# Two attentions of an eight-layer forward pass: order of scores, projections and last down products

## What is computed

```python
# differential attention: 8 heads, two score maps each, head width 64, value width 128
s = einsum(q, k) * scale + bias            # blocks of 128 queries; mask by chunks of 64
p = softmax(s)
o = (p[0] - lam * p[1]) @ v
o = rmsnorm(o, sub_g) * (1 - lambda_init)
y = o @ w_out
# stick-breaking attention: 16 heads of 64; keys and values from a norm of their own
z = q @ k.T / 8                            # strictly causal
log1m = where(mask, -softplus(z), 0)
a = exp(log_sigmoid(z) + sum of log1m to the right)
y = (a @ v) @ w_o
```

## Time and profile before

| | us |
|---|---|
| median of 3 runs | 1122.97 (1122.48 to 1123.53) |
| the profiled execution | 1124.0 |
| its span, first to last instruction | 1122.1 |
| TensorE busy in it | 1086.4 (97%) |
| VectorE busy | 757.3 (67%) |
| ScalarE busy | 633.9 (56%) |
| POOL busy | 127.8 (11%) |
| mean granted clock of TensorE | 0.991 |

### The profile page before, as it was taken

How to read it: one execution, slowest core, us unless ns; L and a number is a source line. 1 busy time by engine, 2 the same in 40 slices (tenths; PEclk the granted TensorE clock), 3 DMA queues, 4 the chain that set the end, 5 groups by cost and what they waited for, 6 DMA issues and landing times.

```text
span 1122.1 us, 15867 instructions
## 1 busy us (share of the span) xinstructions
PE 1086.4 (97%) x6474; PEld 949.8 (85%) x6474; DVE 757.3 (67%) x883; ACT 633.9 (56%) x848; POOL 127.8 (11%) x131
## 2 busy tenths in 40 slices
PE   9999999999999989999997999999999998999997
PEld 8979888887899788888876888888899878888886
DVE  6877876767776668766767765656675546755554
ACT  7656755656555656665565343435568765443532
POOL 0001332120021164312200000000000000000000
PEclk9999999999999989999999999999999999999999
DMA  9836676553544455555542556464363333655551
GB/s 345 307 123 238 221 253 216 168 183 138 192 152 146 150 207 174 204 185 187 192 146 76 207 192 220 160 216 169 132 225 126 104 113 145 213 183 197 178 187 38
DMA packets 31143, 202.23 MB, mean 180 GB/s; under 512 B 3640, under 2 KB 3808, under 8 KB 8544
## 3 DMA queue, kind: packets, MB, share of 16 engines
q1 hardware_dynamic: 28032, 189.16, 48.0%
q0 software_dynamic: 3040, 12.07, 3.2%
HBM read 200.15 MB, written 2.63 MB: 181 GB/s over the span
## 4 chain that ended last, share of the span: by engine, by line
PE 78%; DVE 11%; ACT 4%; issue 3%; POOL 2%; DMA 1%; SPq 0%; DVEq 0%; ACTq 0%; POOLq 0%
PE wk L621 20%; PE wk L623 10%; PE acc L595 8%; PE acc L597 8%; PE acc L596 8%; PE wk L644 4%; DVE w_lo L296 4%; PE wk L595 3%; PE wk L597 3%; PE wk L596 3%; ACT w_hi L287 2%; PE wk L653 1%; DVE x L1469 1%; DVE region L1663 1%; PE acc L779 1%
## 5 line engine op out<-in xcount | busy, mean ns | idle before, releaser
L296 DVE TENSOR_TENSOR w_lo<-raw,w_hi 128x2048 fp32r<-128x2048 f32 x168 | 384.3, 2292 | 74.6 <-ACT w_hi L287 68.6
L621 PE MATMUL wk<-a_hl,w_hi 128*128 128x512 f32 x1024 | 365.2, 400 | 3.7 <-DVE region L1771 1.9
L287 ACT ACTIVATE w_hi<-raw 128x2048 fp32r<-128x2048 f32 x173 | 329.5, 1907 | 13.2 <-DMA raw<-ws 12.5
L623 PE MATMUL wk<-a_hl,w_lo 128*128 128x256 f32 x1024 | 288.0, 281 | 0.0
L621 PEld LDWEIGHTS wk<-a_hl,w_hi 128*128 128x128 f32 x1024 | 193.1, 189 | 52.5 <-DVE region L1653 3.2
L623 PEld LDWEIGHTS wk<-a_hl,w_lo 128*128 128x128 f32 x1024 | 194.1, 190 | 1.5
L595 PE MATMUL acc<-w_hi,b_hl 128*128 128x512 f32 x432 | 169.4, 392 | 1.3 <-DVE w_lo L296 1.3
L596 PE MATMUL acc<-w_lo,b_hl 128*128 128x512 f32 x432 | 168.5, 390 | 0.0
L597 PE MATMUL acc<-w_hi,b_hl 128*128 128x512 f32 x432 | 168.4, 390 | 0.0
L1363 ACT ACTIVATE region<-wk 128x512 f32<-128x512 f32 x30 | 17.9, 596 | 159.8 <-PE wk L623 156.5
L595 PEld LDWEIGHTS acc<-w_hi,b_hl 128*128 128x128 f32 x432 | 81.1, 188 | 19.6 <-DVE w_lo L296 2.1
(11 more groups left out here) (258 smaller groups left out, 1653.7 us busy)
## 6 DMA issues: line engine op xcount, KB each, us to landing
raw<-ws SPq DMA_DIRECT2D x173, 1024.0 KB, 4.9
gain<-gains POOLq DMA_DIRECT2D x13, 512.0 KB, 4.8
raw<-ws SPq DMA_DIRECT2D x8, 256.0 KB, 6.2
region<-rows SPq DMA_DIRECT2D x1, 1664.0 KB, 9.7
lines_dram<-line_dram POOLq DMA_DIRECT2D x1, 1536.0 KB, 8.7
bias<-gains POOLq DMA_DIRECT2D x3, 512.0 KB, 6.9
region<-xT SPq DMA_DIRECT2D x4, 256.0 KB, 5.0
x<-x_rows SPq DMA_DIRECT2D x1, 1024.0 KB, 7.2
```

What stands on the lines that cost most here:

```text
L287: act.activation(w_hi[:, u % HIGH, :], raw[:, u % RAW, :], ACT.Copy).then_inc(hi_ready, 1)
L296: dve.tensor_tensor(w_lo[:, u % LOW, :], raw[:, u % RAW, :], w_hi[:, u % HIGH, :].bitcast(F32), ALU.subtract).then_inc(lo_ready, 1)
L621: pe.matmul(banks[:, m, :], wh[:, k, c], a_hl[:, k, :, :].rearrange("p e t -> p (e t)"), start=k == 0, stop=False, skip_group_check=True)
L623: mm = pe.matmul(banks[:, m, T:2 * T], wl[:, k, c], a_hi[:, k, :], start=False, stop=k == DT - 1, skip_group_check=True)
```

## The change

- **Scores inside the value projections.** In both attentions the scores stand in the middle of a value unit and no longer behind it; units are cut with `feat_part` and `token_part`. Differential attention's first round has an order of its own (`diff_first`): scores(0) ahead of the low products of v, scores(1) in the middle of the next query unit. VectorE's and ScalarE's lists are rewritten to it.
- **Queries of four heads first.** Stick-breaking attention takes its units in the order q0, q1, k0, v0, k1, v1, q2, k2, v2, q3, k3, v3 (`STICK_UNITS`), and its junction prepares the keys' input later.
- **Last four downs by token halves.** `down_tokens` does one half of the tokens of a down unit; half 0 of all four comes before half 1 of the last three. The low part of the last unit of each attention goes to spare memory (`SPARE`). `by_threes` now holds for these junctions too, so half 0 is turned ahead of the last half unit, and the low split of the next sublayer's first unit moves from ahead of the junction into it.
- **Mean squares without divisions.** With den the sum of exponentials, the old steps computed (ss / den / den / 128 + eps) ^ -0.5 / den on POOL in five instructions. The new ones compute (ss / 128 + eps den^2) ^ -0.5, two on VectorE and the power on POOL.

The diff, cut to its core:

```diff
+STICK_UNITS = (("q", 0), ("q", 1), ("k", 0), ("v", 0), ("k", 1), ("v", 1), ("q", 2), ("k", 2), ("v", 2), ("q", 3),
+               ("k", 3), ("v", 3))
+STICK_MID = {3: 0, 4: 1, 5: 2, 6: 3, 8: 4, 9: 5}
+STICK_END = {10: 6, 11: 7}
...
+        SPARE = {U_DIFF + 15: o_lo_t[:, :, :].rearrange("p k t -> p (k t)"),
+                 U_STICK + 15: b_hl[:, 0:DT // 2, :, :].rearrange("p k e t -> p (k e t)")}
+        def low_of(u):
+            return SPARE[u] if u in SPARE else w_lo[:, u % LOW, :]
...
+            if u == U_STICK + 15:
+                dve.wait_ge(unit_done, U_STICK + 12)
+            elif u >= LOW and u not in SPARE:
...
-            return n not in (J_DIFF, J_POOL, J_STICK)
+            return n != J_POOL
...
-                pool.wait_ge(o_squared, 4 * (j + 1))
-                over = rden[:, :, :].rearrange("p e (n m) -> p e n m", m=2)[:, :, :, 0]
-                four = lambda t: t[:, c].rearrange("p (e n) -> p e n", e=2)
-                pool.tensor_tensor(four(o_ms), four(o_ss), over, ALU.mult).then_inc(o_mean, 1)
-                pool.wait_ge(o_mean, 4 * j + 1)
-                pool.tensor_tensor(four(o_ms), four(o_ms), over, ALU.mult).then_inc(o_mean, 1)
-                pool.wait_ge(o_mean, 4 * j + 2)
-                pool.tensor_scalar(o_ms[:, c], o_ms[:, c], 1.0 / P, EPS, ALU.mult, ALU.add).then_inc(o_mean, 1)
-                pool.wait_ge(o_mean, 4 * j + 3)
-                pool.tensor_tensor(o_rs[:, c], o_ms[:, c], minus_half[:, :], ALU.pow).then_inc(o_mean, 1)
-                pool.wait_ge(o_mean, 4 * j + 4)
-                pool.tensor_tensor(four(o_rs), four(o_rs), over, ALU.mult).then_inc(o_rms, 1)
+                pool.wait_ge(o_mean, 2 * j + 2)
+                pool.tensor_tensor(o_rs[:, c], o_ms[:, c], minus_half[:, :], ALU.pow).then_inc(o_rms, 1)
...
+            def down_tokens(n, u, h, pair, res, first=False):
+                last = u == LAST[n]
+                if h == 0:
+                    pe.wait_ge(lo_ready, u + 1)
+                for f in range(2):
+                    for kk in range(2):
+                        mm = down_half(u, h, kk, f, *pair, res, first and kk == 0, last and kk == 1)
+                    if last:
+                        mm.then_inc(unit_done if h and f else res_done, 1)
+                if h and not last:
+                    mm.then_inc(unit_done, 1)
...
+            def diff_first(base):
+                half_pair(base, wk[:, 0:2, :], J_FFN0, 0)
+                half_pair(base + 1, wk[:, 2:4, :], J_FFN0, 0)
+                turn_half(J_FFN0, 1)
+                half_token(base + 2, acc[:, 3, :], J_FFN0, 0, a_hi, a_lo)
+                half_pair(base, wk[:, 0:2, :], J_FFN0, 1)
+                low_pair(base, wk[:, 0:2, :])
+                half_pair(base + 1, wk[:, 2:4, :], J_FFN0, 1)
+                low_pair(base + 1, wk[:, 2:4, :])
+                half_token(base + 2, acc[:, 3, :], J_FFN0, 1, a_hi, a_lo)
+                pe.wait_ge(dq_ready, 1)
+                pe.wait_ge(dk_ready, 1)
+                diff_scores(0)
+                low_token(base + 2, acc[:, 3, :], a_hi)
+                feat_part(base + 3, 0, range(0, 4))
+                pe.wait_ge(dv_ready, 2)
+                diff_scores(1)
+                feat_part(base + 3, 0, range(4, DT))
+            diff_first(U_DIFF)
             for j in range(1, 4):
-                projections(U_DIFF, j, 0, dreleased)
-                outputs_pair(j - 1)
-                projections(U_DIFF, j, 1, dreleased)
+                u = U_DIFF + 3 * j
+                if j > 1:
+                    pe.wait_ge(dq_ready, j)
+                    feat_part(u, 0, range(DT))
+                pe.wait_ge(dk_ready, j)
+                if j > 1:
+                    outputs_pair(j - 1)
+                    feat_part(u + 1, 1, range(DT))
+                else:
+                    diff_turn(0)
+                    feat_part(u + 1, 1, range(0, 4))
+                    diff_av(0)
+                    diff_turn(1)
+                    feat_part(u + 1, 1, range(4, 6))
+                    diff_av(1)
+                    feat_part(u + 1, 1, range(6, DT))
+                pe.wait_ge(dv_ready, 2 * j)
+                token_part(u + 2, 2, 0, range(0, 4), a_hi, a_lo)
                 diff_back(j - 1)
-                projections(U_DIFF, j, 2, dreleased)
-                scores_pair(j)
-            pe.wait_ge(dv_ready, 8)
-            unit_down(U_DIFF + 12, *b_pair(0), True, res=wk)
+                token_part(u + 2, 2, 0, range(4, DT), a_hi, a_lo)
+                pe.wait_ge(dq_ready, j + 1)
+                pe.wait_ge(dk_ready, j + 1)
+                diff_scores(2 * j)
+                diff_scores(2 * j + 1)
+                token_part(u + 2, 2, 1, range(DT), a_hi, a_lo)
+            u = U_DIFF + 12
+            down_tokens(J_DIFF, u, 0, b_pair(0), wk, True)
+            down_tokens(J_DIFF, u + 1, 0, b_pair(1), wk)
             outputs_pair(3)
-            unit_down(U_DIFF + 13, *b_pair(1), False, res=wk)
+            down_tokens(J_DIFF, u + 2, 0, b_pair(2), wk)
             diff_back(3)
-            last_downs(J_DIFF, U_DIFF + 14, (b_pair(2), b_pair(3)), (None, (o_lo, 8)), res=wk)
+            down_tokens(J_DIFF, u, 1, b_pair(0), wk, True)
+            pe.wait_ge(o_lo, 8)
+            down_tokens(J_DIFF, u + 3, 0, b_pair(3), wk)
+            down_tokens(J_DIFF, u + 1, 1, b_pair(1), wk)
+            down_tokens(J_DIFF, u + 2, 1, b_pair(2), wk)
+            turn_half(J_DIFF, 0)
+            down_tokens(J_DIFF, u + 3, 1, b_pair(3), wk)
...
+            def stick_first(base):
+                q0, q1, k0 = wk[:, 0:2, :], wk[:, 2:4, :], acc[:, 2:4, :]
+                half_pair(base, q0, J_MLP0, 0)
+                turn_half_kv(0)
+                half_pair(base + 1, q1, J_MLP0, 0)
+                pe.wait_ge(blo_ready, 2)
+                turn_half(J_MLP0, 1)
+                half_pair(base + 2, k0, J_MLP0, 0, b_hl, True)
+                half_pair(base, q0, J_MLP0, 1)
+                turn_half_kv(1)
+                low_pair(base, q0)
+                half_pair(base + 1, q1, J_MLP0, 1)
+                low_pair(base + 1, q1)
+                half_pair(base + 2, k0, J_MLP0, 1, b_hl, True)
+                low_pair(base + 2, k0, b_hi)
...
+            for c in range(3, 12):
+                if c == 3:
+                    pe.wait_ge(sq_ready, 2)
+                stick_unit(c, 0)
+                if c in STICK_MID:
+                    stick_there(STICK_MID[c])
+                    stick_step(STICK_MID[c])
+                stick_unit(c, 1)
+                if c in STICK_END:
+                    stick_there(STICK_END[c])
+                    stick_step(STICK_END[c])...
+                if n == J_MLP0:
+                    split_hi(act, last + 3)
                 if by_threes(n):
                     input_hi(0)
                 result_squares(1)
                 if not by_threes(n):
                     input_hi(0)
+                x_squares(1)
                 if n == J_MLP0:
                     kv_hi(0)
-                x_squares(1)
-                if n == J_FFN1:
+                    input_hi(1)
...
-            for j in range(4):
+            low_copy(U_DIFF, wk[:, 0:2, :], diff_low[:, 0, :, :], d_low)
+            low_copy(U_DIFF + 1, wk[:, 2:4, :], diff_low[:, 1, :, :], d_low)
+            split_hi(act, U_DIFF + 3)
+            diff_exp(0)
+            split_hi(act, U_DIFF + 4)
+            token_copy(U_DIFF + 2, 0, 3, av, ACT.Copy, dv_ready, src=acc)
+            diff_exp(1)
+            split_hi(act, U_DIFF + 5)
+            for j in range(1, 4):
...
-                token_copy(u + 2, j, 2 if j else 3, av, ACT.Copy, dv_ready, src=wk if j else acc)
-                split_hi(act, u + 2 + CUT)
+                diff_o_hi(j - 1)
                 diff_exp(2 * j)
                 diff_exp(2 * j + 1)
+                token_copy(u + 2, j, 2, av, ACT.Copy, dv_ready)
+                split_hi(act, u + 2 + CUT)
...
-                if n == J_MLP0:
-                    kv_lo(0)
                 if not by_threes(n):
                     input_lo(0)
                 next_input(1)
                 if n == J_MLP0:
+                    kv_lo(0)
+                input_lo(1)
+                if n == J_MLP0:
                     kv_input(1)
-                input_lo(1)
...
+                dve.scalar_tensor_tensor(out=four(o_rs), in0=under, scalar=EPS, in1=under, op0=ALU.mult, op1=ALU.mult)                   .then_inc(o_mean, 1)
...
+                dve.scalar_tensor_tensor(out=four(o_ms), in0=four(o_ss), scalar=1.0 / P, in1=four(o_rs), op0=ALU.mult,
+                                         op1=ALU.add).then_inc(o_mean, 1)
...
-            for j in range(4):
+            feat_sum(wk[:, 0:2, :], diff_low[:, 0, :, :], d_low, 1, qT[:, 0:2, :], dq_ready)
+            split_lo(dve, U_DIFF + 3)
+            feat_sum(wk[:, 2:4, :], diff_low[:, 1, :, :], d_low, 2, kT[:, 0:2, :], dk_ready)
+            diff_bias(0)
+            split_lo(dve, U_DIFF + 4)
```

(19 more changed lines are left out.)

## The result

| | before | after |
|---|---|---|
| median of the runs, us | 1123.25 (1122.48 to 1124.06, 4 runs) | 1134.76 (1133.18 to 1136.95, 4 runs) |
| ratio, 95% interval | | 1.0105 (1.009 to 1.012) |
| profiled execution, us | 1124.0 | 1136.95 |
| its span | 1122.1 | 1135.1 |
| mean granted clock | 0.991 | 0.986 |

The change makes the kernel 11.5 us slower. Forecast was 6.2 slower with 1133 as upper end: the sign was right, the time 5.6 us too low and outside the range.

The account below looks back on a forecast made before the run. TensorE, busy 1086.4 of 1122.1 us, bounds the kernel; only the other 36 us and low-clock time can be had. Terms 9.0 - 1.4 - 4.9 + 1.1 + 1.3 + 2.1 - 5.0 + 4.0 = +6.2, median 1129.2, range 1121 to 1133.

Parts of the forecast that it names:

- a, first round: First round of differential attention: lists bind link by link, new TensorE waits sum to 12.0 us; net +9.0 (+6 to +10).
- b: Rounds 2 and 3 of differential attention: L878 waits go, rounds of 22.0 instead of 22.8; -1.4 us (-2.2 to 0).
- c: Last downs of differential attention by token halves: the stop before L644 goes; -4.9 us (-5.3 to -4).
- d: First units of feed-forward 1: clock gain -2.05, but late POOL band work delays the gate, 3.0 waiting; +1.1 us.
- e, junction: Junction before stick-breaking attention: TensorE idles 2.6 us for the keys' low part before the second half's turn; +1.3 us net.
- e, end: End of stick-breaking attention: last low part of output behind the spare low split +1.2 us; stop and slow clock go, -5.0.
- f, clock: Clock falls behind new idle places: three of four uncovered ones at 1.3 us each; +4.0 us (0 to +7).
- Rival 3: Whole kernel: slower by POOL's late band work in feed-forward 1 only, costing 5 to 6 us, total 1133; chance 0.14.
- Rival 2: Whole kernel: the change does what it says, lists don't bind, all stops go, 1106 to 1114 us; chance 0.06.

Follow-up runs that it names:

- e10: The kernel before, with the last downs by token halves and the mean squares without divisions: 1120.86 us, ratio 0.9969 to the kernel before.
- e7: The kernel before, with only the last four downs of both attentions by token halves: 1119.07 us, ratio 0.9968 to the kernel before.
- e15: e12 without the token halves, the last four down units of both attentions as in the kernel before: 1123.61 us, ratio 1.0004 to the kernel before.
- e2: The changed kernel, with VectorE's low part of output 6 ahead of the low split of unit 142 in stick-breaking attention: 1130.20 us.
- e13: The changed kernel, with POOL's band work in pieces and its five loads of gain rows, both behind the gates of feed-forward 1: 1130.44 us.
- e1: The changed kernel, with VectorE's key sum of pair 0 ahead of the low split of unit 48 in differential attention: 1131.85 us.
- e3: The changed kernel, with e1's move and ScalarE's and VectorE's lists in differential attention's first round reordered as data come free: 1123.24 us.
- e9: The changed kernel, with 30 empty products ahead of TensorE's wait before the last value products of stick-breaking attention: 1133.01 us.
- e12: The changed kernel, with orders mended in both attentions and the junction, POOL's band work spread and its gain loads behind the gates: 1109.25 us.
- e5: The changed kernel, with only POOL's band work cut into seven pieces, one behind each gate of feed-forward 1: 1133.25 us.

## Why the prediction was right in sign and too low

The letters are the prediction's terms.

- **a, first round.** Forecast waits 3.65, 1.9 or slow clock in its place, 2.2, 0.3, 3.9; measured 3.75, 0.4 and 1.3 lost to slow clock, 2.06, 0, 3.78, with the releasers forecast. Walking the lists in order gave each within 0.3 us.
- **b.** The third round took 22.2 us for 22.8 before, the second 23.7 with a fall of the clock in it. Right. That POOL's divisions mattered in it is not shown: e10 says that their part alone gives nothing.
- **c.** From the last pair's scores to feed-forward 1 it is 31.45 us with half a v unit of 2.9 in it, before 33.12 without: 4.6 for the 4.9 forecast. But the forecast took the term for one that stands alone; e7 (4.2 us alone) and e15 (14.4 with the rest and mended lists) show that it needs the rest. That it is the earlier scores which it needs is argued from the rows, not shown apart.
- **d.** First units 19.85 us, forecast 19.84. POOL's work ended 29.1 us after the feed-forward's start, as forecast (at 433.5, since the start was 3.7 later than forecast), and the gate stood right behind it. TensorE's wait was 2.73, forecast 3.0, but the cause named was wrong: it came a unit earlier, from longer VectorE instructions and a late weight load, in a place where the kernel before already waited 1.54, which the term should have taken off. "SP's loads keep their order" was true and not enough: POOL's loads moved toward them. That the size agreed is chance.
- **e, junction.** 2.44 for 2.6, key sum 1.04 for 1.1, first cumulated sum 0.66 for 0.4. Right.
- **e, end: the step that failed.** "The last low part of the output behind the spare low split +1.2". The low split was seen, but the wait was priced for output 7 and the last unit's half 0. The one that binds is output 6: the value products of step 9 wait for its low part, VectorE's split ahead of that waits for ScalarE's high split, and this stands behind a table load (1.28), an exponential and the high part. The wait was 4.33 us, 3.1 more than forecast, and it drew 2.4 of slow clock behind it. With this one order mended (e2) the kernel takes 1130.2, inside the range; it gave back 4.6 us in the median and 6.0 in the trace.
- **f, clock, mis-sized beside it.** Taken as three falls of 1.3 us. There were five beyond the covered one. Against the same products in a run whose clock stayed up there they cost 1.5, 1.5, 1.6 and 1.7 us and, behind the missed wait, 2.4 for a stretch twice as long: 8.7 for 4.0. With the 3.1 of the wait that is 7.8 too much; 1.5 is balanced by the wait that d should have taken off, and 0.5 is not placed. The kernel before had shown the size: its fall at 607.4, behind a wait of 2.6 us in the pooling stage, which the term left out, cost 1.7. The profiled execution came out 6.8 over the forecast for such a one, the median 5.6.
- **Rivals.** Rival 3 (POOL, 1133) came near the right time for the wrong reason: with POOL mended alone (e13) the kernel still takes 1130.4. Rival 2 (the change does what it says) was given 6%: with mended lists it is what happens, at 1109.

## What to carry to other kernels

- When work on one engine is moved earlier, write down for each of its inputs what stands ahead of it in the other engines' lists. A large instruction that is not urgent (here a split of 2.3 us that itself waits for another engine) must not stand ahead of a short one that TensorE waits for. A handful of moved lines made 25 us here.
- Price a wait at the first step that waits on its semaphore, not at the step that reads the data. Mending one link of such a chain moves the stop on (e1); the chain must be walked to its end (e3).
- Parts of a change can need each other (e7, e10, e15). A part that gives little alone is not shown to be worthless, nor the reverse.

## What the runs showed of the hardware

- A wait of TensorE of over 3 us cost up to 2.4 us more behind it in clock, and 30 empty products in one of 4.2 us saved that (e9: clock 1.00 for 0.50).
- A wait of 2.0 to 2.6 us in the attentions and junctions was followed by slow clock in 10 cases of 14, in one run and not in another of the same order, so a forecast of it needs a range.
- A multiply of 128 x 4 elements on POOL took 2.18 us beside a low split of VectorE, and VectorE's taps 2.28 for four beside POOL's work and 1.79 without (e13).
- Five loads of 512 KB from POOL's queue under way beside them raised the 1 MB weight loads from 4.9 (e12) to 8.4 us (e5).
